# Latent tokens ordered by grid columns, and value tiles evicted one by one, in a hybrid attention and retention step

## The reference

```python
NA_ROWS = 8
NA_COLS = 16
...
    kr = min(NA_ROWS, rows)
    kc = NA_COLS
...
    c0 = jnp.clip(cidx - kc // 2, 0, GRID_W - kc)
    in_win = (cidx[None, :] >= c0[:, None]) & (cidx[None, :] < c0[:, None] + kc)
...
    bias = rpb[:, dr[:, None, :, None], dc[None, :, None, :]].astype(jnp.float32)
...
    s_win = jnp.where(in_win[None, None, None, :, None, :], s_win, -jnp.inf)
    s_ctx = jnp.einsum('brchd,bkhd->bhrck', qg, k_ctx).astype(jnp.float32) * scale
    nwin = kr * GRID_W
    s = jnp.concatenate([s_win.reshape(B, H, rows, GRID_W, nwin), s_ctx], axis=-1)
    p = jax.nn.softmax(s, axis=-1).astype(v.dtype)
```

## Time and profile before

| what | value |
|---|---|
| median of 3 runs | 3338.84 us |
| the profiled execution's own time | 3333.62 us |
| its span | 3331.8 us |
| mean granted TensorE clock | 0.984 of full speed |
| TensorE busy | 3244.8 us (97%) |
| VectorE, ScalarE, GpSimd busy | 1474.4, 902.6, 287.1 us |
| chain that ended last | TensorE 89%, VectorE 3%, issue 2%, ScalarE 2%, DMA 2% |
| neighbourhood attention, first score to output projection | 719.4 to 843.1 us |

### The profile page before, as it was taken

How to read it: one execution, slowest core, us unless ns; L and a number is a source line. 1 busy time by engine, 2 the same in 40 slices (tenths; PEclk the granted TensorE clock), 3 DMA queues, 4 the chain that set the end, 5 groups by cost and what they waited for, 6 DMA issues and landing times.

```text
span 3331.8 us, 49560 instructions
## 1 busy us (share of the span) xinstructions
PE 3244.8 (97%) x20192; PEld 2989.2 (90%) x20192; DVE 1474.4 (44%) x2057; ACT 902.6 (27%) x1278; POOL 287.1 (9%) x365
## 2 busy tenths in 40 slices
PE   8899999999999999999999999999999999999999
PEld 5899999976868999999999999868687786999999
DVE  3564634257554564633662434443352524422223
ACT  3111213334354321213311213321222222321221
POOL 1000001012001000001000001030210204000001
PEclk8999999999999999999999999999999999999999
DMA  8443422221101443422342222212122121222222
GB/s 201 160 146 126 145 70 76 75 73 29 59 1 51 145 147 125 152 89 76 121 157 89 95 70 76 87 64 70 63 83 70 57 82 35 66 71 72 79 70 70
DMA packets 84777, 299.37 MB, mean 90 GB/s; under 512 B 10383, under 2 KB 12719, under 8 KB 83984
## 3 DMA queue, kind: packets, MB, share of 16 engines
q1 hardware_dynamic: 57888, 206.77, 18.9%
q0 software_dynamic: 20560, 73.84, 8.2%
q10 hardware_dynamic: 6176, 16.54, 1.4%
HBM read 289.62 MB, written 8.44 MB: 89 GB/s over the span
## 4 chain that ended last, share of the span: by engine, by line
PE 89%; DVE 3%; issue 2%; ACT 2%; DMA 2%; POOL 1%; SPq 0%; ACTq 0%; DVEq 0%; POOLq 0%
PE ps L1210 36%; PE ps L1193 30%; PE ps L1386 11%; PE ps L1440 2%; PE ps L1235 2%; PE ps L1595 2%; PE ps L1415 2%; PE ps L1604 1%; ACT tmp_g L499 1%; DMA ada<-in_ada 1%; PE ps L1428 1%; PE ps L1583 1%; PE ps L1243 1%; DMA mhalf<-in_mhalf 1%; PE ps L1248 1%
## 5 line engine op out<-in xcount | busy, mean ns | idle before, releaser
L1210 PE MATMUL ps<-h,w 128*128 128x320 f32 x8640 | 1291.6, 311 | 23.0 <-DVE w L787 12.9
L1210 PEld LDWEIGHTS ps<-h,w 128*128 128x128 f32 x8640 | 1279.1, 189 | 30.1 <-DVE w L787 14.2
L1193 PE MATMUL ps<-g,w 128*128 128x320 f32 x5376 | 802.4, 310 | 8.5 <-DVE g L1156 8.5
L1193 PEld LDWEIGHTS ps<-g,w 128*128 128x128 f32 x5376 | 795.1, 189 | 9.8 <-issue 9.8
L787 DVE TENSOR_TENSOR w<-raw,w 128x1024 fp32r<-128x1024 f32 x383 | 461.0, 1224 | 294.3 <-ACT w L474 290.4
L1386 PE MATMUL ps<-w,h 128*128 128x512 f32 x1596 | 369.5, 391 | 5.5 <-ACT rv L729 3.1
L474 ACT ACTIVATE w<-raw 128x1024 fp32r<-128x1024 f32 x207 | 215.8, 1060 | 550.4 <-PE ps L1193 444.4
L1386 PEld LDWEIGHTS ps<-w,h 128*128 128x128 f32 x1596 | 297.7, 188 | 70.9 <-issue 4.7
L882 DVE TENSOR_TENSOR tmp_g<-tmp_s,ps 128x640 f32<-128x640 f32 x88 | 72.3, 821 | 601.2 <-ACT tmp_s L515 601.2
L515 ACT ACTIVATE tmp_s<-ps 128x640 f32<-128x640 f32 x88 | 62.1, 705 | 901.9 <-PE ps L1210 901.9
L805 DVE SCALAR_TENSOR_TENSOR acc<-ada,sc,acc 128x1024 f32<-128x1024 f32 x224 | 273.8, 1278 | 1.5 <-DMA ada<-in_ada 1.5
(11 more groups left out here) (160 smaller groups left out, 1970.5 us busy)
## 6 DMA issues: line engine op xcount, KB each, us to landing
raw<-in_ws SPq DMA_DIRECT2D x383, 512.0 KB, 3.7
ada<-in_ada POOLq DMA_DIRECT2D x132, 512.0 KB, 4.0
ada<-in_ada ACTq DMA_DIRECT2D x6, 1024.0 KB, 17.1
rst<-in_state ACTq DMA_DIRECT2D x4, 1024.0 KB, 5.0
out_new_state<-rsx ACTq DMA_DIRECT2D x8, 512.0 KB, 2.6
bias<-rp_rep POOLq DMA_DIRECT2D x16, 224.0 KB, 4.2
x<-in_xT SPq DMA_DIRECT2D x1, 2560.0 KB, 25.9
rp_rep<-in_rpb POOLq DMA_DIRECT2D x1, 930.0 KB, 40.1
```

The source lines that it names most:

```text
L1193: mm = pe.matmul(pair_half(pr, half, width), w2[:, slot, wi, at:at + cols], rhs(k, ri)[:, half * width:(half + 1) * width], start=(k == 0 ...
L1210: mm = pe.matmul(pair_half(pr, half), w2[:, n % RING, wi, k * P:(k + 1) * P], h2[:, k, ri, half * HT:(half + 1) * HT], start=(k == 0 and w ...
```

## The change

Latent tokens are stored by columns: the host transposes `x_sample` to columns first, and 16 columns by 8 rows make a tile of 128 queries. The keys of such a tile are 24 columns (192 keys, b = 1 and 4) or 32 columns (256 keys, b = 2 and 3), plus the 128 cached ones. Scores, exponential and sums run over 320 or 384 keys where they ran over 640; there are three transposes and three value products a latent unit. The scale of the context keys is part of the sum with the bias, whose columns there are zero. The latent attention's tables of angles follow the new order; its work stays. Because windows begin in the middle of a tile, six value tiles are made (token offsets in `V_AT`), in banks 2 to 7, and tiles in banks 6 and 7 wait for `c_n` 5, the normalised latent keys. The first score stands behind the third of the four value blocks; each value tile signals `v_mm` and is evicted alone. Biases come laid out by the host, 128x256 a head, and GpSimd adds the mask in three sums; the DMA of 64 copies is gone. In the retention layer, `norm_hi` reads its latent input by steps of 8 elements and writes rows, and `add_to_x` reads and writes `x` by steps of 8.

```diff
-V_BANK = [2, 3, 4, 5, 0]
+V_BANK = [2, 3, 4, 5, 6, 7]
...
+V_AT = [0, NCTX, NCTX + 64, NCTX + 192, NCTX + 320, NCTX + 384]
+V_OF = [None, 0, 1, 2, 3, 5]
+NA_WINDOW = {1: (0, 192), 2: (64, 256), 3: (192, 256), 4: (320, 192)}
+NA_CHUNKS = {1: [(0, 0, 0, P), (64, 1, 64, P), (192, 4, 0, P)],
+             2: [(0, 1, 0, P), (128, 2, 0, P), (256, 4, 0, P)],
+             3: [(0, 2, 0, P), (128, 3, 0, P), (256, 4, 0, P)],
+             4: [(0, 3, 0, 64), (64, 5, 0, P), (192, 4, 0, P)]}
...
+RET_NORM = 4
...
+def by_rows(ap):
+    return ap.rearrange("p (r c) -> p r c", c=GRID_W)
...
+def by_columns(ap):
+    return ap.rearrange("p (c r) -> p r c", r=ROWS)
...
-            pool.dma_start(a["rp_rep"].rearrange("r (e w) -> r e w", w=RPW),
-                           a["rpb"].rearrange("r (o w) -> r o w", o=1).to_broadcast([NAH * RPR, RP_REP, RPW])
-                           ).then_inc(rp_rep, 16)
...
+            def rows_load(h):
+                pool.dma_start(rows[:, h % 2, :], a["rpb"][h]).then_inc(rows_ld[h % 2], 16)
+            rows_load(0)
             for h in range(NAH):
+                if h + 1 < NAH:
+                    if h >= 1:
+                        pool.wait_ge(bias_rdy, h)
+                    rows_load(h + 1)
                 if h >= 2:
                     pool.wait_ge(s_neg, 5 * (h - 2) + 4)
-                for r2 in range(2):
-                    src = bass.AP(a["rp_rep"].tensor, (h * RPR + 1 - r2) * RP_REP * RPW + NA_COLS - 1,
-                                  [[RPW - 1, GRID_W], [RP_REP * RPW, 14], [1, GRID_W]])
-                    pool.dma_start(bias[64 * r2:64 * r2 + 64, h % 2, :].rearrange("p (j n) -> p j n", n=GRID_W),
-                                   src).then_inc(bias_ld[h % 2], 16)
-                pool.wait_ge(bias_ld[h % 2], 32 * (h // 2 + 1))
-                b3 = bias[:, h % 2, :].rearrange("p (j n) -> p j n", n=GRID_W)
-                pool.tensor_tensor(b3, b3, colmask.rearrange("p (o n) -> p o n", o=1).to_broadcast([P, 14, GRID_W]),
-                                   ALU.add).then_inc(bias_rdy, 1)
+                pool.wait_ge(rows_ld[h % 2], 16 * (h // 2 + 1))
+                r3 = rows[:, h % 2, :].rearrange("p (n r) -> p n r", r=ROWS)
+                for b, n0, n1, m0 in ((1, 8, 32, 0), (2, 0, 32, 24), (4, 0, 24, 56)):
+                    n = n1 - n0
+                    dst = bias[h % 2][:, NA_BIAS[b]:NA_BIAS[b] + n * ROWS].rearrange("p (n r) -> p n r", r=ROWS)
+                    ins = pool.tensor_tensor(dst, r3[:, n0:n1, :],
+                                             colmask[:, m0:m0 + n].rearrange("p (n o) -> p n o", o=1)
+                                             .to_broadcast([P, n, ROWS]), ALU.add)
+                ins.then_inc(bias_rdy, 1)
...
-                    for part, st in ((ctx_of, 0), (lat_of, 1)):
-                        ins = act.activation(part(tmp_g[:, k % 2, :]), part(tmp_s[:, k % 2, :]), ACT.Identity,
+                    for st in range(2):
+                        dst, src = ((ctx_of, lat_of)[st](u[:, k % 2, :]) for u in (tmp_g, tmp_s))
+                        if nn == RET_NORM and st:
+                            dst, src = by_rows(dst), by_columns(src)
+                        ins = act.activation(dst, src, ACT.Identity,
...
-            act.wait_ge(wt_free, done(n0 + 17))
-            act.dma_start(va[:, 4, :], a["cache_v"]).then_inc(em_ld3, 16)
-            for t in range(NT):
-                act.activation(va[:, 5 if t == 0 else t - 1, :], ps[:, V_BANK[t], :], ACT.Copy).then_inc(v_ev, 1)
-            act.wait_ge(v_ev, NT)
-            act.dma_start(a["new_v"], va[:, 5, :]).then_inc(out_done, 16)
+            act.wait_ge(wt_free, done(n0 + 13))
+            act.dma_start(va_na[4], a["cache_v"]).then_inc(em_ld3, 16)
...
+            exp_unit(0, True)
+            act.wait_ge(em_kr, 1)
+            for t in range(len(V_AT)):
+                if t < len(V_AT) - 1:
+                    act.wait_ge(v_mm, t + 1)
+                else:
+                    act.wait_ge(wt_free, done(n0 + 17))
+                act.activation(va_ctx if t == 0 else va_na[V_OF[t]], ps[:, V_BANK[t], :], ACT.Copy
+                               ).then_inc(v_ev, 1)
+            act.wait_ge(v_ev, 1)
+            act.dma_start(a["new_v"], va_ctx).then_inc(out_done, 16)
...
-                for part, st in ((ctx_of, 0), (lat_of, 1)):
-                    ins = dve.scalar_tensor_tensor(part(x[:, m, :]), part(pair(pr)),
-                                                   g[:, m, st:st + 1], part(x[:, m, :]), ALU.mult, ALU.add)
+                for st in range(2):
+                    dst, src = ((ctx_of, lat_of)[st](u) for u in (x[:, m, :], pair(pr)))
+                    if rows and st:
+                        dst, src = by_columns(dst), by_rows(src)
+                    ins = dve.scalar_tensor_tensor(dst, src, g[:, m, st:st + 1], dst, ALU.mult, ALU.add)
...
-                    at = (6 - 2 * (b - 1)) * GRID_W
-                    dve.scalar_tensor_tensor(sbs[g % 3][:, 0:NLAT], src[:, 0:NLAT], NAD ** -0.5,
-                                             bias[:, h % 2, at:at + NLAT], ALU.mult, ALU.add)
-                    link(dve.tensor_scalar(sbs[g % 3][:, NLAT:T], src[:, NLAT:T], NAD ** -0.5, None, ALU.mult))
-                    dve.tensor_reduce(nm, sbs[g % 3], AX.X, ALU.max, negate=True).then_inc(s_neg, 1)
+                    nk, at = keys_of(b, na), NA_BIAS[b]
+                    link(dve.scalar_tensor_tensor(sbs[g % 3][:, 0:nk], src[:, 0:nk], NAD ** -0.5,
+                                                  bias[h % 2][:, at:at + nk], ALU.mult, ALU.add))
+                    dve.tensor_reduce(nm, sbs[g % 3][:, 0:nk], AX.X, ALU.max, negate=True).then_inc(s_neg, 1)
...
+                            if k == ktot - 1 and tile_done is not None and t != tiles[-1]:
+                                mm.then_inc(tile_done, 1)
...
-            def v_wait(t):
-                pe.wait_ge(em_ev, 13)
-                if V_BANK[t] == 0:
-                    pe.wait_ge(em_kr, 1)
-            tok_tiles(n0 + 14, 4, of_h, KD, range(NT), lambda t: V_BANK[t], v_wait)
...
-                    pe.matmul(ps[:, 2 * (g % 2), :], lhs, lat_of(k[:, PAST:]),
-                              start=True, stop=True)
-                    mm = pe.matmul(ps[:, 2 * (g % 2) + 1, 0:P], lhs, k[:, 0:PAST], start=True, stop=True)
+                    w0, nw = NA_WINDOW[b] if na else (0, NLAT)
+                    sc_out = bank2(g % 2)
+                    pe.matmul(sc_out[:, 0:nw], lhs, lat_of(k[:, PAST:])[:, w0:w0 + nw], start=True, stop=True)
+                    mm = pe.matmul(sc_out[:, nw:nw + PAST], lhs, k[:, 0:PAST], start=True, stop=True)
...
-                for kt in range(1 if b == 0 else 5):
-                    mm = pe.transpose(bank2(2)[:, kt * P:(kt + 1) * P], src[:, kt * P:(kt + 1) * P], ident)
+                at = [0] if b == 0 else [c[0] for c in NA_CHUNKS[b]] if na else [kt * P for kt in range(5)]
+                for kt, c in enumerate(at):
+                    mm = pe.transpose(bank2(2)[:, kt * P:(kt + 1) * P], src[:, c:c + P], ident)
...
+                    for kt, (_, tile, k0, k1) in enumerate(NA_CHUNKS[b]):
+                        mm = pe.matmul(ps[r0:r0 + 64, 6, (b - 1) * P:b * P], va_na[tile][k0:k1, h * 64:h * 64 + 64],
+                                       pt[k0:k1, kt, (b - 1) * P:b * P], start=(kt == 0), stop=(kt == 2))
...
-            pe.wait_ge(em_ld, 16)
+            def v_wait(t):
+                pe.wait_ge(em_ev, 12 if t < 2 else 13)
+                if V_BANK[t] >= 6:
+                    pe.wait_ge(c_n, 5)
+            def first_scores(u):
+                if u == 2:
+                    pe.wait_ge(em_kr, 1)
+                    pe.wait_ge(em_ld, 16)
+                    score_mm(0, True)
+            tok_tiles(n0 + 14, 4, of_h, KD, range(len(V_AT)), lambda t: V_BANK[t], v_wait,
+                      lambda ap, t: ap[:, V_AT[t]:V_AT[t] + P], first_scores, v_mm)
             pe.wait_ge(em_ld3, 16)
-            pe.wait_ge(v_ev, NT)
-            pe.wait_ge(c_n, 5)
             attend(0, NU, True)
...
-    xt = np.concatenate([w["x_prompt"][0], w["x_sample"][0]])
+    grid = w["x_sample"][0].reshape(ROWS, GRID_W, D).transpose(1, 0, 2).reshape(NLAT, D)
+    xt = np.concatenate([w["x_prompt"][0], grid])
```

More of the change, by code:

```diff
@@ L76 @@
 EM_X, RET_X = 24, 88
-RPW = 2 * NA_COLS - 1
-RPR = 2 * NA_ROWS - 1
-RP_REP = 64
 NEG = -1.0e30
@@ L178, in build @@
         ka = over("ka", 4 * (PAST + T), ada_at).rearrange("p (k t) -> p k t", k=4)
-        bias = over("bias", 2 * 14 * GRID_W, ada_at).rearrange("p (a c) -> p a c", a=2)
+        bias0 = over("bias0", NA_BIAS_COLS, ada_at)
+        rows = over("rows", 2 * NA_SPAN, ada_at).rearrange("p (a c) -> p a c", a=2)
+        el[0] += 1024
         esq = place("esq", 2 * T, at=el[0]).rearrange("p (a t) -> p a t", a=2)
@@ L1162, in _ @@
                     for m in (2 * j, 2 * j + 1):
```

(20 more changed lines are left out.)

70 lines of the change are left out of this document (47 added, 23 removed).

## The result

In nine runs each, the changed kernel took 3345.62 us (3339.67 to 3346.44) and the kernel before 3336.63 us (3334.48 to 3339.93): a ratio of 1.0021, 95% interval 1.0012 to 1.003. It is slower by 7 us (by the ratio) to 9 us (by the medians), where 44.6 us less had been forecast. (The 3338.84 us that the forecast started from are the median of the first three of the nine runs of before.) The profiled execution spans 3343.4 us against 3331.8, so 11.6 us are to be found.

The account below looks back on a forecast made before the run. TensorE, holding 89% of the chain that ended last, was taken as the bound. The terms -11.0 + 7.5 - 41.1 = -44.6 us, from 3338.8, gave 3294 us; range 3282 to 3309.

Parts of the forecast that it names:

- The start: Modulation weights near the kernel's start: without the 64-fold bias copy, TensorE's 9.67 us idle and a clock loss go, -11.0 us.
- The value projection: Value products before attention: 24 more products cost 5.5 us and a wait for the normalised keys 2.0, +7.5 us.
- The neighbourhood attention: From last value product to output projection: TensorE-bound heads with 1.6 us of waits each, 85.9 us against 127.0, -41.1 us.
- at full clock: Neighbourhood attention: unit times taken at full clock give 8.84 us of TensorE work a head where it was 13.9.
- The clock stays low: Rival: from the value projection through attention the clock falls to 1.2 GHz and does not rise, 3398 us; chance 0.03.
- The start of attention: Before attention's first transposes: early scores overlap the value products, leaving 2.4 us of TensorE idle time, bounds 1.5 and 8.
- The rest: ScalarE, bias loads, memsets and retention's 8-element steps: 0 us, steps 12.3 at most; rival of slow steps 3300 us, chance 0.13.
- The feeding chain: Rival in attention: each unit's chain of scores, exponential, product and transposes makes TensorE wait 3 us a head, 3305 us; chance 0.17.

Follow-up runs that it names:

- `e4_before_host_copies`: The kernel before with the 64 copies of the bias table laid out by the host, so that DMA goes: 3325.94 us, ratio 0.9973.
- `e12_high_clock`: Also experiment 6: the changed kernel plus sixteen unread products, five and three at attention's start, one in each of the next eight units: 3293.1 us, ratio 0.9868.
- experiment 1: Also `e1_fill_start`: the changed kernel plus 8 unread products in the two gaps at attention's start, five and three: 3335.05 us, ratio 0.9982.
- 4: The changed kernel plus five and three unread products at attention's start and one in each of the other 38 units: 3300.1 us, ratio 0.9887.
- 5: `e8_columns_out` with the extra product per unit in the first two heads only, the start's five and three kept: 3286.82 us, ratio 0.9864.
- `e3_no_steps`: The changed kernel with `norm_hi` and `add_to_x` run without steps, so retention scans tokens by grid columns: 3335.87 us against 3345.62.
- `e8_columns_out`: The kernel of 4 with retention output transposed into PSUM in grid-column order, so `add_to_x` has no steps: 3295.23 us, 4.9 below it.
- `e6_burst`: The changed kernel plus one block of 16 unread products before head 2's first transposes: five runs 3311.04 to 3317.16 us, five 3343.73 to 3353.07.

## Why the prediction was wrong

- **The start**: -11.0 forecast, -11.75 in the trace, 11.1 in `e4_before_host_copies`. The mechanism is right: with the copy gone the idle time is gone. That the size fits so well is in part luck. At the sums of the first block the changed kernel is 13.1 us ahead (114.68 against 127.76). Of these 1.7 lie ahead of the gap, where the granted clock was 0.71 instead of 0.51 from 43 to 48 us, which nobody had forecast; and 1.3 are lost again by 583 us: behind a wait of 1.76 us that ends at 243.48 the clock was 0.88 and then 0.91 over 16 us, where the kernel before came through the same wait (1.66 us, ending at 256.49) at 1.00.
- **The value projection**: +7.5 forecast, +8.35 measured, with 1.73 us of waiting for the keys where 2.0 were expected. Right.
- **The neighbourhood attention**: -41.1 forecast, +8.4 measured. This is the step that failed, and in it the clock. With the clock at 1.00 throughout, the stage takes 84.4 us (`e12_high_clock`), with up to 4 us of extra products in it, against the forecast's 85.9. That the two lie so close is luck: the work of a head was 1.0 us too low and its waits 1.15 us too high, and the errors cancel. What failed is the sentence "at full clock", put on work whose clock the change itself decides. The rival *The clock stays low* had the mechanism, though not the place of the fall, and got 0.03.
- The reason against that rival was that TensorE would be busy for 85% of the changed head, and had been for 94% at 1.00 before. That compared only the state at the high level. It was even true there: `e12_high_clock` holds 1.00 with TensorE busy for 47.8 of 50 us. The question was whether the stage, once low, comes back. The earlier trace rows held the warning: 14 us at 0.53 in which TensorE counted as busy for 13.7 of them. At the low level a head of this kind fills 17.4 us of TensorE's time without a wait, and the busy share tells nothing of the clock. Before, the heads brought it back after 14 us; the thinner ones did not in 130 us.
- The rival's price was wrong as well: 104 us for attention and value products together. The fall came behind the value products, and at the low level the work of a head grew from 9.85 to 17.4 us and not to twice its length, so the price was 135.4 - 84.4 = 51 us, barely more than the 44.6 from which the rival decides. That is why the kernel is 7 to 9 us slower and not 60.
- **The start of attention**: 2.4 us of idle time was forecast "at full clock". In the trace it is 1.3 us (0.97 and 0.29 before the first two groups of transposes; 2.7 of 4 us busy), and the fall follows it. Filled, the fall moved (experiment 1), and with products in the units as well it did not come (4, 5, 6).
- **The rest**: 0 was taken for the stepped accesses and 12.3 kept as the bound. Measured 6.6 to 9.7 (`e3_no_steps`), and 4.9 for the additions alone at the high clock (`e8_columns_out`). The Trainium skill (Advanced Engine Details and Errata, section Memory Cachelines) had spoken against the change, and the trace agrees: 1.35 against 0.80 us on ScalarE, 1.25 against 0.74 on VectorE. "I take the nearest row" was a poor choice here, since the nearest row was the very operation without what was in dispute. The same section says that any non-contiguous access pattern in PSUM slows matmuls down significantly; for the fp32 transposes that write 32 bytes apart this case measures otherwise, 273 ns at the median with and without the step.
- The feeding chain was no bound: at the high clock TensorE waited for 0.45 us a head, where 1.6 had been forecast.

Not settled: what tells the runs of `e6_burst` that stay low from those that rise, and the one high run of `e1_fill_start`; each was profiled in one execution only, so no view sets the two kinds side by side.

## What to carry to other kernels

A change that thins a stage's TensorE work can lose its clock: forecast the stage at both levels (here 84 and 135 us), and ask of each entry and each gap which of the two the stage will be in, not only what is saved at the level of before. Where a low level holds in a stage of short products, a few products that nobody reads, at the entry and in the first units, cost at most 4 us here and gave back 51; look for the granted clock of every stage before cutting work further. Where TensorE makes a transpose anyway, try the change of order in its writes first: it cost nothing here, while the ScalarE and VectorE accesses cost 0.5 us for 512 columns.
